# A dilated softmax with its row maximum subtracted on VectorE, and one exponential per 1024 columns

## What is computed

```
m = jnp.max(logits, axis=-1, keepdims=True)
p = jnp.exp(logits - m)
den = jnp.sum(p, axis=-1)
o = jnp.einsum('brnhqk,brnkhd->brnqhd', p, vv) / jnp.swapaxes(den, -1, -2)[..., None]
lse = jnp.swapaxes(m[..., 0] + jnp.log(den), -1, -2)
...
wts = jax.nn.softmax(jnp.stack(lses, 0), axis=0)
return jnp.sum(wts[..., None] * jnp.stack(outs, 0), axis=0)
```

## Time and profile before

| what | value |
|---|---|
| median of 3 runs | 1489.6 us (1487.02 to 1493.04) |
| the profiled execution: its own time | 1487.59 us |
| its span | 1485.8 us |
| TensorE, VectorE, ScalarE, GpSimd busy | 92%, 42%, 30%, 34% of the span |
| the stage from the end of `nm` to the first matmul of the output projection | 1024.97 to 1057.60 us of the span |

### The profile page before, as it was taken

The page is one execution under the profiler, slowest core; times in us unless marked ns, Lnnn a source line. Parts: engine busy times, 40 slices in busy tenths (PEclk is TensorE's granted clock), DMA queues, the critical chain, the costliest instruction groups (busy, mean ns, idle before and its releaser), DMA issues.

```text
span 1485.8 us, 17068 instructions
## 1 busy us (share of the span) xinstructions
PE 1366.9 (92%) x6510; PEld 1123.3 (76%) x6510; DVE 622.7 (42%) x830; ACT 449.3 (30%) x603; POOL 506.8 (34%) x209
## 2 busy tenths in 40 slices
PE   3799998798999999999899999887889999999995
PEld 3678776588888888888788778656779888887884
DVE  5569751858643433400882232226486111010007
ACT  2343233314233223212323323333233323322121
POOL 2334331024345344444243333100125444444440
PEclk9899998799999999999999999997999999999998
DMA  9493632042556546643235322001113232234311
GB/s 335 134 97 102 212 117 82 22 176 72 181 175 209 197 152 232 182 126 100 104 116 180 109 85 72 29 1 57 36 50 100 99 99 99 92 79 154 99 57 56
DMA packets 93456, 173.79 MB, mean 117 GB/s; under 512 B 15655, under 2 KB 61879, under 8 KB 93276
## 3 DMA queue, kind: packets, MB, share of 16 engines
q1 hardware_dynamic: 90264, 169.63, 36.8%
q10 hardware_dynamic: 3140, 3.43, 0.9%
HBM read 170.87 MB, written 4.52 MB: 118 GB/s over the span
## 4 chain that ended last, share of the span: by engine, by line
PE 64%; issue 22%; DVE 6%; POOL 6%; ACT 2%; POOLq 0%; DVEq 0%; ACTq 0%
PE ps L1018 12%; PE ps L1020 12%; PE ps L1019 12%; PE ps L1050 6%; PE ps L1051 6%; PE ps L1052 6%; POOL w_lo L670 6%; PE ps L1462 1%; PE ps L1143 1%; PE ps L1145 1%; PE ps L1144 1%; PE ps L1434 1%; PE ps L1445 1%; PE ps L1448 1%; DVE rec L2101 1%
## 5 line engine op out<-in xcount | busy, mean ns | idle before, releaser
L670 POOL TENSOR_TENSOR w_lo<-raw,w_hi 128x1024 fp32r<-128x1024 f32 x205 | 506.6, 2474 | 943.8 <-ACT w_hi L690 943.4
L1018 PE MATMUL ps<-h_lo,w_hi 128*128 128x512 f32 (+2 forms) x1064 | 401.6, 377 | 13.6 <-DVE tmp L1867 6.2
L1019 PE MATMUL ps<-h_hi,w_hi 128*128 128x512 f32 (+2 forms) x1064 | 398.0, 374 | 0.0
L1020 PE MATMUL ps<-h_hi,w_lo 128*128 128x512 f32 (+2 forms) x1064 | 397.4, 374 | 0.0
L690 ACT ACTIVATE w_hi<-raw 128x1024 fp32r<-128x1024 f32 x205 | 216.0, 1056 | 487.8 <-PE ps L1052 189.0
L1018 PEld LDWEIGHTS ps<-h_lo,w_hi 128*128 128x128 f32 (+1 forms) x1064 | 204.1, 192 | 54.4 <-DVE tmp L1867 7.5
L1020 PEld LDWEIGHTS ps<-h_hi,w_lo 128*128 128x128 f32 (+1 forms) x1064 | 203.9, 192 | 35.1
L1019 PEld LDWEIGHTS ps<-h_hi,w_hi 128*128 128x128 f32 (+1 forms) x1064 | 203.9, 192 | 34.0
L1951 DVE TENSOR_TENSOR tmp<-tmp,ps 128x512 f32<-128x512 f32 x44 | 30.1, 688 | 264.2 <-PE ps L1020 264.2
L1050 PE MATMUL ps<-w_hi,hid_lo 128*128 128x512 f32 x352 | 137.9, 392 | 1.8 <-issue 0.9
L1052 PE MATMUL ps<-w_lo,hid_hi 128*128 128x512 f32 x352 | 137.5, 390 | 0.0
(11 more groups left out here) (228 smaller groups left out, 1491.5 us busy)
## 6 DMA issues: line engine op xcount, KB each, us to landing
raw<-wstream SPq DMA_DIRECT2D x205, 512.0 KB, 4.1
ada_raw<-astream SPq DMA_DIRECT2D x80, 512.0 KB, 4.6
ada_first<-astream SPq DMA_DIRECT2D x12, 512.0 KB, 10.0
ln_rows<-row_scratch SPq DMA_DIRECT2D x3, 1024.0 KB, 6.8
skew_scratch<-f_scratch ACTq DMA_DIRECT2D x1, 2304.0 KB
ada_first<-astream SPq DMA_DIRECT2D x8, 256.0 KB, 4.6
xa<-xT SPq DMA_DIRECT2D x4, 512.0 KB, 9.4
out<-xa SPq DMA_DIRECT2D x4, 512.0 KB, 3.5
```

What stands on the lines that cost most here:

```text
L670: nc.gpsimd.tensor_tensor(w_lo[:, slot, :], raw[:, slot % RAW, :], w_hi[:, slot, :].bitcast(F32), ALU.subtract).then_inc(sem("w_lo_ready"), 1)
L1018: pe.matmul(o, w_h, x_l, start=start, stop=False)
L1019: pe.matmul(o, w_h, x_h, start=False, stop=False)
L1020: return pe.matmul(o, w_l, x_h, start=False, stop=stop)
```

## The change

VectorE now adds `nm` to the logits itself, one instruction for a head and kind (128 x 1024, in place, the column of each tile t repeated over its 256 keys), and ScalarE takes one exponential over the 1024 columns without a bias. `dil_exp` waits for VectorE's new semaphore `dil_less` in place of `nm_ready`. VectorE does the two additions of head 0 first, and each later one ahead of one of its copies: (1,0) ahead of the copy of round 1, (1,1) ahead of 3, (2,0) ahead of 5, (2,1) ahead of 7, (3,0) ahead of 9 and (3,1) ahead of 11.

```
@@ -984,11 +984,9 @@
         def dil_exp(h, kind):
-            act.wait_ge(sem("nm_ready"), 1)
-            for t in range(TB):
-                i = nc.scalar.activation(lgs[kind][:, h, t, :], lgs[kind][:, h, t, :], ACT.Exp,
-                                         bias=nm[:, kind, TB * t + h:TB * t + h + 1])
-            i.then_inc(sem("dil_p"), 1)
+            act.wait_ge(sem("dil_less"), 2 * h + kind + 1)
+            rows_ = lgs[kind][:, h, :, :].rearrange("q t x -> q (t x)")
+            nc.scalar.activation(rows_, rows_, ACT.Exp).then_inc(sem("dil_p"), 1)
@@ -2102,7 +2100,18 @@
+        def less_max(h, kind):
+
+            rows_ = lgs[kind][:, h, :, :]
+            V.tensor_tensor(rows_, rows_, nm[:, kind, h:16:TB].unsqueeze(2).to_broadcast([P, TB, 256]), ALU.add
+                            ).then_inc(sem("dil_less"), 1)
+
+        dve.wait_ge(sem("nm_ready"), 1)
+        less_max(0, 0)
+        less_max(0, 1)
         for n in range(1, 16, 2):
+            if n // 4 + 1 < 4:
+                less_max(n // 4 + 1, n % 4 // 2)
             dve.wait_ge(sem("turn_full"), n + 1)
```

## The result

The changed kernel takes 1493.83 us (median of 22 runs, 1489.66 to 1496.2), the kernel before 1487.92 us (22 runs, 1484.33 to 1493.04). The ratio is 1.0036 with a 95% interval of 1.0025 to 1.0046: slower by 5.4 us (3.7 to 6.8), less than 0.5% of the time.

The account below looks back on a forecast made before the run. VectorE's list from the first reciprocal on was taken to end the stage; 0.6 + 3.5 - 0.4 + 0.5 = +4.2 us on a median of 1489.6 gave 1493.8 us, range 1488.5 to 1499.

Parts of the forecast that it names:

- 1, head: Start of the stage: first turn waits for an addition, a semaphore and the wide exponential, 2.34 - 1.70 = +0.6 us.
- 2, five additions under cover: Ahead of the first reciprocal: five additions fall into VectorE's waits or finish ahead of need, costing 0.
- 3, three additions in the chain: Between first reciprocal and low part: additions (2,1), (3,0), (3,1) on VectorE cost 3 x 1.16 = 3.5 us.
- 3, the wait ahead of the second reciprocal: VectorE's 0.43 us of waiting for product 7 goes: -0.4 us.
- 4, high part: Before VectorE's subtraction: ScalarE's last exponential and high part follow addition (3,1), a new VectorE wait of 0.45, say +0.5 us.
- 5, the end: Fourth reciprocal still waits some 1.0 us for product 15, the 4.22 us before the output projection stays: 0.
- The first: Rival: TensorE's clock falls within the stage, slowing matmuls and product 15; in all +6.0 us, 1495.6 us; chance 0.30.
- The second: Rival: VectorE's additions run at the one-operand price, 749 ns; +2.3 us, 1491.9 us; chance 0.05.
- third: Rival: VectorE and GpSimd hinder each other at every addition, 2275 ns each; +9.0 us, 1498.6 us; chance 0.05.
- The fourth: Rival: ScalarE sets the pace, each shorter exponential bringing 0.64 us; even all eight -5.1 us, 1484.5 us; chance 0.03.
- an early or late rise: TensorE's clock rising earlier or later in the stage's first half: 1.3 us either way if off by 2.6 us.

Follow-up runs that it names:

- the exponentials alone: The kernel before with one exponential of 1024 columns in place of four and no additions; ratio 0.9987 (0.9970 to 1.0003).
- the second series: The changed kernel run again, unchanged, for a second profile and a closer ratio against the kernel before; ratio 1.0032 (1.0017 to 1.0048).

## Why the prediction was right

The forecast was 1493.8 us and +4.2 us; measured are 1493.83 and +5.4 (3.7 to 6.8), of which the stage holds 4.0. That the median agrees is luck: the forecast started from a median of three runs of before, 1489.6, which 22 runs put at 1487.92; a start 1.7 us too high and a change 1.2 us too small nearly cancelled. The steps:

| step | forecast | measured |
|---|---|---|
| 1, head | first turn +0.6, first reciprocal +0.6 | +0.62, +0.51 |
| 2, five additions under cover | 0 | 0, waits of 0.94, 1.59, 0.97 us left |
| 3, three additions in the chain | +3.5 | 1.13 + 1.13 + 1.26 = +3.52 |
| 3, the wait ahead of the second reciprocal | -0.4 | -0.43 |
| 4, high part | +0.5 | +0.32 |
| 4, product 11 at the low clock | none | +0.10 |
| 5, the end | 0 | 0 |
| sum | +4.2 | +4.02 (36.66 - 32.63 = 4.03) |

Step 4 was a little off in kind: behind the new wait a second one, for product 11, ends last, because the clock had fallen by the end of TensorE's wait of 2.46 us for the copy of round 11.

The rivals. The first came about as a mechanism and not at its price: the clock fell, in all four profiles of the changed kernel, but only for some 3.4 us (from about 1054.7 to 1058.1). It charged 0.1 us ahead of the third reciprocal and 1.2 us to the cover of product 15; the 0.7 us for product 15 itself never came, since the clock was back. The second and third fell with the addition's 1216 ns and GpSimd's 0.00 us. The third was priced too low, though: the 2275 ns are a mean over two kinds. Of the twelve additions in that row, in the trace of the kernel before, six took 1.22 or 1.23 us with GpSimd idle and six 3.26 to 3.39 with GpSimd at work. At 3.3 us an addition the forecast's own sum gives 2.7 + 9.6 - 0.4 + 0.5 = 12.4, some 1502 us, above the range; this is an estimate that no run tests. The fourth fell with the exponentials alone: tail unchanged.

What was left out of the working is the spread of the first half: the forecast allowed 1.3 us either way for an early or late rise, and took the profile of before as typical, where half of its kind are 1.5 us shorter. That is one candidate for the 1.4 us between the stage's 4.0 and the kernel's 5.4.

The other lies ahead of the stage. `nm` ended at 1024.97, 1022.78, 1028.89 and 1027.00 us in the profiles of before, at 1029.57, 1030.05, 1028.19 and 1030.25 in those of the changed kernel, and between 1022.7 and 1027.8 in the six others. The code up to there is the same in all, and before alone spreads over 6.1 us. The granted clock goes with it. Added up over stretches of 10 us, it was low for 88, 88, 101 and 94 us ahead of `nm` in the profiles of before and for 101, 101, 95 and 101 in those of the changed kernel; over all fourteen profiles `nm` comes 0.45 us later for each us more of it (correlation 0.93). Much of the difference lies between 200 and 300 us of the span. Its busy time (columns as in rows 2), in the second profile of before and in the second of the changed kernel:

```profile
200.00:300.00 100.00, 85.44 (x439) 65.25 (x438) 52.44 (x139) 36.99 (x72) 17.20 (x8) 0.90 0.18 56
200.00:300.00 100.00, 83.54 (x401) 62.48 (x400) 47.86 (x136) 34.84 (x70) 13.89 (x6) 0.81 0.14 43
```

So `nm` is late where the clock was low for longer in stages that the change doesn't touch. Why that was so in all four profiles of the changed kernel stays open. Two of its profiled executions were not typical of it: 1496.20 us is the longest of its 22, and 1496.63 the second longest of its 12 in the second series, where the medians are 1493.83 and 1493.85. On the whole kernel it can't be much: the interval of the ratio, 3.7 to 6.8 us, leaves up to 2.8 us above the stage's 4.0.

## What to carry to other kernels

Ask which engine's list ends the stage before moving work between engines, and from which instruction on: here an addition cost nothing ahead of VectorE's first reciprocal (but for the very first, which the first exponential waits for) and some 1.14 us behind it, and moving three copies off VectorE paid where moving eight additions onto it cost. Instruction overhead saved on an engine that waits is no gain. A wait of TensorE that hides one thing can be eaten up by another, here by its own clock, before it shows in the time. And a mean duration in a group of rows can hide two kinds of instruction: look at the shortest and the longest before taking it as a price.

## What the runs showed of the hardware

- Dropping the bias column of an activation took it from 497 to 404 ns at 256 columns and from 1.15 to 1.06 us at 1024, 0.09 us in both. Over four narrow exponentials that is 0.37 of the 0.64 us that they take longer than one wide one.
- The Trainium skill, "ScalarE: Activation LUTs" (What ACT_TABLE_LOAD costs), states about 93 ns for each such column operand; these traces agree.
- The same kernel's stage was 31.2 or 32.5 to 32.8 us long by where TensorE's granted clock rose, 4.6 or 7.4 to 7.9 us after `nm`, with nothing changed in the program. A single profile of a stage that starts at the low clock is uncertain by that much; the tail, measured from the first reciprocal, repeated to 0.02 us in each of the two kernels profiled four times.
- TensorE waited 2.44 us ahead of product 11 in the kernel with three additions that nobody waits for, and the granted clock stayed at 1.00; after a wait of 2.46 us at the same place it was at 0.50 in all four profiles of the changed kernel.
- An fp32 addition of 1024 columns with both operands in SBUF took 1.22 or 1.23 us with GpSimd idle and 3.26 to 3.39 where GpSimd ran beside it (six each, in the trace of the kernel before).
